# Issuing the value product of an attention step one step after its transposes

## What is computed

```python
h = rmsnorm(x, g_mix)
z = h @ w_in                          # qA,kA,vA | qB,kB,vB | gate ; 16 heads of 64 in all
# heads 0..7: dilated causal windows with ALiBi, three branches mixed by their softmax denominators
# heads 8..15: causal softmax with the logit bias c[t]-c[s], c = cumsum(log sigmoid(gate))
# for every head and every block of 128 queries:
s = q_block @ k.T / 8 + bias + mask   # 128 x (up to 1024)
p = exp(s - rowmax(s))
o = (p @ v) / rowsum(p)               # the "value product", then the scaling
x = x + concat(o_A, o_B) @ w_out
```

## Time and profile before

| | us |
|---|---|
| median of 3 runs | 1686.51 |
| the profiled execution, its own time | 1687.19 |
| its span, first to last instruction | 1685.2 |
| PE busy | 1629.2 (97%) |
| DVE busy | 880.5 (52%) |
| ACT busy | 641.9 (38%) |
| attention pairs 0 to 7 | about 77 to 625 of the span |
| TensorE's granted clock, mean | 0.987 of full |

### The profile page before, as it was taken

How to read it: one execution, slowest core, us unless ns; L and a number is a source line. 1 busy time by engine, 2 the same in 40 slices (tenths; PEclk the granted TensorE clock), 3 DMA queues, 4 the chain that set the end, 5 groups by cost and what they waited for, 6 DMA issues and landing times.

```text
span 1685.2 us, 22889 instructions
## 1 busy us (share of the span) xinstructions
PE 1629.2 (97%) x8424; PEld 1386.7 (82%) x8424; DVE 880.5 (52%) x1544; ACT 641.9 (38%) x1074; POOL 121.8 (7%) x228
## 2 busy tenths in 40 slices
PE   5999999999999799999999999999999999999997
PEld 5788888888888688898888887888888878888886
DVE  6544434434444443663254165555555567676876
ACT  5445545445554552331044043333333331212122
POOL 0000000000000000000000001333333330000000
PEclk9999999999999899999999999999999999999998
DMA  5201010111110232052111012666666798676753
GB/s 167 55 26 28 26 28 15 26 28 27 27 27 15 83 101 91 26 150 75 50 38 50 26 50 88 212 212 213 212 214 219 257 363 324 240 262 210 263 188 150
DMA packets 152962, 204.84 MB, mean 122 GB/s; under 512 B 8192, under 2 KB 93312, under 8 KB 152864
## 3 DMA queue, kind: packets, MB, share of 16 engines
q1 hardware_dynamic: 134960, 144.95, 26.1%
q0 software_dynamic: 17920, 58.73, 9.9%
HBM read 140.61 MB, written 63.57 MB: 121 GB/s over the span
## 4 chain that ended last, share of the span: by engine, by line
PE 88%; DVE 4%; ACT 3%; DMA 2%; issue 2%; SPq 0%; DVEq 0%; ACTq 0%
PE psG L664 16%; PE psG L647 12%; PE psG L649 12%; PE psG L648 12%; PE psS L1019 8%; PE psO L810 7%; PE psO L1019 4%; PE psG L1019 4%; PE psS L759 4%; PE psG L741 3%; PE psS L676 2%; PE psS L675 2%; PE psS L945 1%; DMA act_hi<-op_rows 1%; PE psS L692 1%
## 5 line engine op out<-in xcount | busy, mean ns | idle before, releaser
L647 PE MATMUL psG<-act_hi,w_hi 128*128 128x512 f32 (+1 forms) x656 | 256.0, 390 | 5.0 <-DVE act_lo L1320 4.7
L648 PE MATMUL psG<-act_lo,w_hi 128*128 128x512 f32 (+1 forms) x656 | 255.1, 389 | 0.0
L649 PE MATMUL psG<-act_hi,w_lo 128*128 128x512 f32 (+1 forms) x656 | 255.0, 389 | 0.0
L810 PEld LDWEIGHTS psO<-V,pT 128*128 128x128 f32 x1152 | 149.8, 194 | 16.0 <-ACT pT L1125 5.6
L1125 ACT ACTIVATE pT<-psS 128x1024 f32<-128x1024 f32 (+7 forms) x128 | 83.6, 653 | 191.1 <-PE psS L759 190.9
L664 PE MATMUL psG<-act_hi,w_lo 128*128 128x512 f32 x360 | 151.3, 420 | 0.0
L639 POOL DMA_DIRECT2D op_rows<-a_hi x112 | 60.8, 543 | 1247.4 <-DVE a_lo L1320 1239.5
L647 PEld LDWEIGHTS psG<-act_hi,w_hi 128*128 128x128 f32 x656 | 124.4, 190 | 30.7 <-DVE act_lo L1320 5.2
L664 PE MATMUL psG<-act_hi,w_hi 128*128 128x512 f32 x360 | 149.3, 415 | 0.0
L810 PE MATMUL psO<-V,pT 128*128 128x64 f32 x1152 | 146.0, 273 | 2.8 <-ACT pT L1125 2.7
L664 PE MATMUL psG<-act_lo,w_hi 128*128 128x512 f32 x360 | 146.2, 406 | 0.0
(11 more groups left out here) (201 smaller groups left out, 3105.5 us busy)
## 6 DMA issues: line engine op xcount, KB each, us to landing
act_hi<-op_rows SPq DMA_DIRECT2D x38, 1024.0 KB, 7.3
op_rows<-a_hi POOLq DMA_DIRECT2D x112, 256.0 KB, 2.8
op_rows<-a_lo POOLq DMA_DIRECT2D x112, 256.0 KB, 3.3
act_lo<-op_rows SPq DMA_DIRECT2D x18, 1024.0 KB, 7.4
raw<-in_w_up_dram SPq DMA_DIRECT2D x32, 512.0 KB, 4.7
raw<-in_w_in_dram SPq DMA_DIRECT2D x22, 512.0 KB, 3.9
qB<-in_w_down_dram SPq DMA_DIRECT2D x8, 1024.0 KB, 9.9
act_late<-in_w_down_dram SPq DMA_DIRECT2D x8, 1024.0 KB, 12.1
```

The lines of the kernel that those rows point to most:

```text
L647: nc.tensor.matmul(dst, sh, mh, start=(k == 0), stop=False)
L648: nc.tensor.matmul(dst, sh, ml, start=False, stop=False)
L649: mm = nc.tensor.matmul(dst, sl, mh, start=False, stop=(k == n - 1))
L810: mm = nc.tensor.matmul(psO[:, u % 2, 0:HEAD], pT[:, b * P:(b + 1) * P], V[par][:, b, h * HEAD:(h + 1) * HEAD], start=(b == 0), stop=(b == ...
```

## The change

The value product of step `u` is issued after the transposes of step `u+1`, and not after its own: in the list, `PV, u-1` stands where `PV, u` stood, step 0 has none, and `PV, 15` is put at the end of the pair. `pT` becomes two buffers that take turns. The reciprocal on DVE moves from the `PV` event to the `T` event, with a further wait for the scaling of two steps before. The second `pT` buffer lies in SBUF that is free at that time. Nothing else is touched: neither `SPLIT_AT` nor the sharing out of `G` in `gaps`.

```diff
@@ pair_steps
-            if part == 0:
-                order.append(("PV", u))
+            if part == 0 and u:
+                order.append(("PV", u - 1))
+    order.append(("PV", STEPS - 1))
     return order
@@ buffers
-    pT = at("pT", [P, T], f32, 126)
+    pT = [at(f"pT{i}", [P, T], f32, 126 + 4 * i) for i in range(2)]
@@ PE, PV
-                            mm = nc.tensor.matmul(psO[:, u % 2, 0:HEAD], pT[:, b * P:(b + 1) * P],
+                            mm = nc.tensor.matmul(psO[:, u % 2, 0:HEAD], pT[u % 2][:, b * P:(b + 1) * P],
@@ ACT, T
-                        nc.scalar.activation(pT[:, 0:n], psS[u % 2][:, 0:n], ACT.Copy).then_inc(pT_done, 1)
+                        nc.scalar.activation(pT[u % 2][:, 0:n], psS[u % 2][:, 0:n], ACT.Copy).then_inc(pT_done, 1)
@@ DVE
-                    elif kind == "PV":
+                    if kind == "T":
                         i = slice(u % 2, u % 2 + 1)
                         dve.wait_ge(exp_done, p * 16 + (u + 1))
+                        if p * 16 + u >= 2:
+                            dve.wait_ge(o_out, p * 16 + u - 1)
                         nc.vector.reciprocal(row_inv[:, i], row_sum[:, i]).then_inc(inv_done, 1)
+                    if kind == "PV":
+                        i = slice(u % 2, u % 2 + 1)
                         dve.wait_ge(inv_done, p * 16 + (u + 1))
                         dve.wait_ge(pv_done, p * 16 + (u + 1))
```

## The result

The changed kernel takes 1708.33 us, the median of 5 runs from 1703.1 to 1709.32; the kernel before, run beside it, 1686.02. The ratio is 1.0125, with a 95% interval from 1.0109 to 1.0142: slower by 22 us. The forecast was 1710.5 with a range from 1699 to 1723. Run once more later, the changed kernel took 1710.72 against 1684.95, ratio 1.016 (1.0141 to 1.0178).

The account below looks back on a forecast made before the run. PE, busy 97% of the span, was taken as the bound. From the profiled 1687.19 us, + 16.8 waits + 9.0 clock drops − 1.5 last pair = 1711.5; the median lies 0.7 lower, so 1710.5 was said, range 1699 to 1723.

Parts of the forecast that it names:

- Part 4: Weight splits tied to PV events: block 2's moves to step 7, PE waits 2.4 us in seven pairs, 16.8; block 3's costs 0.
- Part 5: PE's clock halves behind the new step 7 waits: six drops of seven at 1.5 us, 9.0; bounds 0 and 21.
- Six of six: Evidence for clock drops: behind the first 20 us, each of PE's six idle stretches over 1.6 us was followed by one.
- the prediction's own prices: Cost of clock drops behind loop borders, read from pair times before: 1.5 us in pair 2, 2.3 in pair 4.
- Part 1: Pairs 0 to 6: step 1's wait on the copy goes, PE waits later instead; gain 0 per pair, bounds 0 and 0.5.
- Part 2: DVE: the moved reciprocal and its added wait cost 0, at most 0.2 us a pair were a scaling late.
- Part 3: Last pair, where each product waited for its own copy: 1.5 us gained, bounds a loss of 2 and gain of 4.
- the chain to step 9: Last pair, from step 7's transposes: ACT high parts, DVE low parts, maximum, exponentials take as long as before.
- (a): Rival: the step 7 waits come but the clock doesn't fall, 1702 us; chance 0.17.
- (b): Rival: the clock falls for longer behind the waits, up to 3 us a pair, 1723 us; chance 0.11.
- (c): Rival: no wait for block 2, ACT's high part being done before step 7's copy, 1683 us; chance 0.06.
- (d): Rival: no wait for block 2 and the last pair's holes only move, 1686 us, within 0.2% of before; chance 0.06.

Follow-up runs that it names:

- late-split kernel: Kernel before with only the key block's weight split tied to PV 7, in step 7, value products where they were: 1701.42 us, ratio 1.0107.
- last pair alone: Kernel before with the value product one step late only in the last pair, pairs 0 to 6 unchanged: 1681.79 us, ratio 0.999.
- doubled high part: Changed kernel with ACT making the key block's high part twice, one behind the other: 1720.05 us, 9.3 more than the changed kernel beside it.

## Why the prediction was right

**Part 4, the splits, carried it.** Forecast: a wait of 2.4 in seven pairs, 16.8 us. Measured 2.33, 16.3 us, in the place and with the chain that were named. Putting the split back took the loss away; the split alone, in the old order, brought 17 of the 22 to 26 us.

**Part 5, the clock, was right in kind and its evidence was read too strictly.** Forecast: six drops at 1.5, 9.0 us. Measured: four in one execution, five in another, 1.6 each, 6.4 to 8 us. "Six of six" idle stretches over 1.6 us was a small sample: the waits of 1.6 in the late-split kernel drew three of seven, and the first of the six itself, the 2.37 before 26.10, is there in all 14 traces, with a drop behind it in 8. What I left out is that the drops of before can go away: in the first trace of the changed kernel neither loop border had one. Pair 2 lies at 71.62 with its wait and no drop, where it had 70.48 with a drop and no wait. Fewer drops would also account for the executions at 1703 beside those at 1708 and 1709: their mean granted clocks are 0.987 and 0.990 against 0.985 and 0.986. But only one of these, the one at 1703.68, has a trace.

**How the sum comes out in the profiled execution.** It is 16.5 longer than that of before. Waits + 16.3, four drops + 6.4, the late product's own 0.18 in seven pairs + 1.2, the two borders' drops gone − 1.5 and − 2.3 by the prediction's own prices, their idle time 0.8 shorter, the last pair − 2.0 (pairs 6 and 7 are together 2.1 longer, where a wait, a drop and the 0.18 make 4.1), the stages outside the pairs − 1.0: 16.3. The forecast for this execution was + 24.3, so 8 of it didn't come. That the medians lie near the forecast, + 22.3 and + 25.8 against + 24.0, is in part luck: it rests on how many drops the executions happened to have.

**Part 1** was right: a gain of 0 in pairs 0 to 6. The wait on the copy went and another in front of step 3 came, and with both splits back an undisturbed pair is 0.18 longer, 1.2 us if all seven are alike, which the bounds of the prediction (0 and a gain) didn't hold. **Part 2** was right, no cost. **Part 3** took 1.5 gained. The runs of the last pair alone show 1.7 (−0.2 to 3.4), its trace 3.6, and of these 3.6 only 0.6 is left against a last pair in the old order with as much half clock. The start of step 7's transposes, which I had 1.2 to 3.2 earlier, tells the same. Counted from the pair's start, it stands at 34.75 before, at 31.21 in the late-split kernel, which has the old order but no half clock in steps 5 and 6, and at 29.38 with the late product: 5.4 earlier, of which 3.5 is the clock and 1.8 the product. The step that failed is the one behind it. I had written that the chain to step 9 is as long as before. It was, but PE reached it sooner, so the same chain became a wait of 2.15 in one piece, and that drew a drop.

**The rivals.** (a), no drops, and (b), long ones, are both out in the two traces: four and five drops, all of 3.4 us. The doubled high part shows where (b) begins. (c) and (d) would have needed the split before step 7's copy, and with it there the times are theirs: 1683.

**An expectation that failed on its own** is that of the late split in the old order, 1693 to 1697 against 1701.4. The step was the start of DVE's low part, which I took from ACT's high part alone; in DVE's queue it stood behind a scaling that waits for PE.

## What to carry to other kernels

When an event in a common list is moved, look for everything that is tied to its name, in tables too: here two weight splits moved with the value product, one of them past its deadline, and with it put back no loss was left that could be measured. For every operation that moves, add up the queue ahead of it on each engine that it passes, its waits included, and compare with the time of the first need. A wait taken from an engine that is 97% busy wins nothing unless the work behind it can start sooner too; where it did, in the last pair, the next queue entry ahead of the next need had to be moved as well before the gain could be measured. And where the clock differs from trace to trace, compare stretches that had as much of the half clock: the last pair looked 3.6 us faster, and some 3.0 of it was the clock.

## What the runs showed of the hardware

Idle stretches of TensorE of the same length in the same place of the program are followed by half the clock in one turn and not in another: 3 of 7 at 1.6 us, 4 and 5 of 7 at 2.1, 7 of 7 at 3.2. Other places of the same traces say the same: the first 2.37 us of the earlier trace rows had a drop behind them in 8 of the 14 traces, the last 2.38 (2.37 in the others) in 10, and a wait of 3.44 in the last pair had one at it in all 14. PE's idle time at the border of two loop turns, for which nothing in the profile shows a reason, differs from run to run of one program (1.78 and 2.14 us at the second border in the two traces of before), and with it the clock behind it. Executions of the kernel before lay between 1680 and 1691 us, so that 0.2% here needs many runs.
